# Scan inputs and state products of a hybrid encoder block: one visit of TensorE per block of four array groups, and another split of the PSUM banks

## What is computed

```python
h  = rms_norm(x)
p  = h @ W_in            # [conv x | conv B | conv C | u | gate_a | gate_b]
ya = (B * dwconv3_causal(C * x_conv)) @ W_conv_out
# 32 groups of 16 inputs and 64 complex states:
s_t = A_bar * s_{t-1} + B_bar u_t
yb = GLU(gelu(Re(C s_t) + D u_t))
x  = x + (sigmoid(gate_a) * ya + sigmoid(gate_b) * yb) @ W_o
x  = x + top-2-of-8 experts in the best of 4 groups, of rms_norm(x)
out = rms_norm(x)
```

## Time and profile before

| | us |
|---|---|
| median of three runs | 722.08 |
| lowest, highest | 722.07, 724.77 |
| the profiled execution | 723.69 |
| its span in the trace | 722.0 |
| PE busy, DVE busy in it | 558.9, 206.8 |
| mean granted TensorE clock | 0.89 of full |

### The profile page before, as it was taken

How to read it: one execution, slowest core, us unless ns; L and a number is a source line. 1 busy time by engine, 2 the same in 40 slices (tenths; PEclk the granted TensorE clock), 3 DMA queues, 4 the chain that set the end, 5 groups by cost and what they waited for, 6 DMA issues and landing times.

```text
span 722.0 us, 7544 instructions
## 1 busy us (share of the span) xinstructions
PE 558.9 (77%) x3241; PEld 333.3 (46%) x3241; DVE 206.8 (29%) x443; ACT 70.4 (10%) x132; POOL 39.8 (6%) x68
## 2 busy tenths in 40 slices
PE   8999999999999989899384584566548248457755
PEld 7888888888886646354141141123114014112411
DVE  4799886959512144000010010000001001000002
ACT  3010011111110012100000000000000000000102
POOL 5001111111100011000000000000000000000000
PEclk9999999999999999999796688779679669677889
DMA  9960803363269666999999999999999999999993
GB/s 339 425 268 18 332 1 120 113 242 139 86 270 401 232 235 261 364 432 426 430 428 428 430 427 428 430 428 427 428 429 426 433 428 428 431 426 430 426 426 161
DMA packets 19043, 242.44 MB, mean 336 GB/s; under 512 B 2368, under 2 KB 2496, under 8 KB 4544
## 3 DMA queue, kind: packets, MB, share of 16 engines
q1 hardware_dynamic: 18432, 239.83, 79.8%
q10 hardware_dynamic: 576, 2.10, 0.8%
HBM read 240.87 MB, written 1.05 MB: 335 GB/s over the span
## 4 chain that ended last, share of the span: by engine, by line
PE 54%; DMA 41%; DVE 2%; issue 2%; ACT 0%; POOL 0%; SPq 0%; DVEq 0%; PEldq 0%; POOLq 0%; ACTq 0%
PE bank L1114 27%; DMA ring<-in_w_down 13%; DMA ring<-in_w_gate 12%; PE bank L1364 8%; DMA s_region<-in_w_up 4%; DMA x_region<-in_w_up 4%; PE bank L1372 4%; DMA ring<-in_w_up 4%; PE bank L1246 4%; DMA ring<-in_last_halves 3%; PE bank L1126 2%; PE bank L1413 2%; PE bank L1331 1%; PE bank L1216 1%; PE bank L1231 1%
## 5 line engine op out<-in xcount | busy, mean ns | idle before, releaser
L1364 PE MATMUL bank<-ring,z_region 128*32 128x512 f32 x688 | 118.5, 676 | 63.5 <-DMA ring<-in_w_gate 14.9
L1114 PE MATMUL bank<-x_region,ring 128*128 128x256 f32 x640 | 142.2, 381 | 0.0
L1114 PEld LDWEIGHTS bank<-x_region,ring 128*128 128x128 f32 x640 | 120.4, 190 | 20.9 <-issue 5.1
L1364 PEld LDWEIGHTS bank<-ring,z_region 128*32 128x32 f32 x688 | 33.6, 122 | 123.5 <-issue 123.5
L1372 PE MATMUL bank<-ring,m_region 128*32 128x512 f32 x240 | 55.5, 749 | 26.6 <-DMA ring<-in_w_down 16.0
L1038 DVE TENSOR_TENSOR z_region<-z_region,bank 128x512 f32<-128x512 f32 x8 | 8.2, 1027 | 209.2 <-PE bank L1364 197.1
L1364 PE MATMUL bank<-x_region,z_region 128*32 128x512 f32 x80 | 44.9, 725 | 10.7 <-DMA ring<-in_w_up 10.7
L1042 DVE COPY m_region<-bank 128x512 f32<-128x512 f32 x8 | 5.5, 691 | 139.3 <-PE bank L1372 111.3
L1372 PE MATMUL bank<-s_region,m_region 128*32 128x512 f32 x64 | 36.9, 741 | 8.6 <-DMA ring<-in_w_down 8.6
L1364 PE MATMUL bank<-rot_region,z_region 128*32 128x512 f32 x64 | 37.6, 755 | 6.8 <-DMA ring<-in_w_up 6.8
L1331 PE MATMUL bank<-conv_region,h_region 128*128 128x128 f32 x256 | 33.9, 288 | 4.7 <-issue 4.0
(11 more groups left out here) (240 smaller groups left out, 570.0 us busy)
## 6 DMA issues: line engine op xcount, KB each, us to landing
ring<-in_w_gate SPq DMA_DIRECT2D x26, 2048.0 KB, 34.5
ring<-in_w_up SPq DMA_DIRECT2D x17, 2048.0 KB, 33.8
ring<-in_mix SPq DMA_DIRECT2D x16, 2048.0 KB, 9.7
ring<-in_w_down SPq DMA_DIRECT2D x15, 2048.0 KB, 35.0
ring<-in_first SPq DMA_DIRECT2D x8, 2048.0 KB, 12.6
s_region<-in_w_down SPq DMA_DIRECT2D x4, 2048.0 KB, 36.2
x_region<-in_w_up SPq DMA_DIRECT2D x4, 2048.0 KB, 36.8
rot_region<-in_w_up SPq DMA_DIRECT2D x4, 2048.0 KB, 35.8
```

The costliest lines, as they stand in the source:

```text
L1114: ins = MM(dst, w[:, k, n * P:(n + 1) * P], rhs[:, k, :], start=k == 0, stop=k == kn - 1)
L1364: ins = MM(bank[to][quarter(e), :], xT[:, k, quarter(e)], of_expert[e][:, FF * k:FF * k + FF], start=k == 0, stop=k == KD - 1)
```

## The change

The same products are made, in fewer visits of PE to the scan. Four tables behind mains take the place of the old steps: `array` (scan inputs of a whole block, behind mains 7, 15, 25, 34), `states` (state products of a whole block, behind 20, 26, 35, 45), `behind` (the DVE steps, where they were), `products` (`y_pre` of blocks 0 to 2 behind 22, 31, 40). The gelus of blocks 0 to 2 come behind main 42, and `y_pre` and gelu of block 3 at the very end of the list.

Each visit now has eight products in four array groups: four row groups into banks 4 to 7 (inputs), or four column groups into bank 3 (state products). The projections have banks 0 to 2: x, ga and nearly all gb share bank 0, b and c alternate between 1 and 2, co takes 0, 2, 1 in turn. Six states are kept; two lie where the raw input lay, and the table's scratch moves beside them. The waits follow the banks: x of n = 1, 2 waits for the copy of x(n - 1), x of n > 2 for the sigmoid of gb(n - 3), which stands right before it in the list.

```diff
-S5_LAG = 2
+STATES_KEPT = 6
...
-    order, step = [], 0
+    behind = {7 + t * 9 // 4: ("step", t) for t in range(ST)}
+    products = dict(zip((22, 31, 40), (("ypre", b) for b in range(YB - 1))))
+    array = dict(zip((7, 15, 25, 34), (("bu", b) for b in range(YB))))
+    states = dict(zip((20, 26, 35, 45), (("out", b) for b in range(YB))))
+    order = []
     for g, main in enumerate(mains):
         order.append(main)
-        while step < ST + S5_LAG and g == 7 + step * 9 // 4:
-            order.append(("s5", step))
-            step += 1
-    assert step == ST + S5_LAG
-    return order
+        order += [table[g] for table in (array, states, behind, products) if g in table]
+        if g == 42:
+            order += [("gelu", b) for b in range(YB - 1)]
+    return order + [("ypre", YB - 1), ("gelu", YB - 1)]
...
+        ACT_BANK, Y_BANK, CO_BANKS = 0, 3, (0, 2, 1)
+
+        def conv_bank(j):
+            return 1 + j % 2
+
         def gate_bank(what, n):
 
-            if n + GATE_LAG < KD:
-                return 2 * (n % 2)
-            return 0 if what == "ga" else 2
+            return conv_bank(KD - 2) if what == "gb" and n + GATE_LAG >= KD else ACT_BANK
+
+        def co_bank(n):
+            return CO_BANKS[n % len(CO_BANKS)]
...
+        def state(t):
+
+            t %= STATES_KEPT
+            return s_first[:, t] if t < 4 else s_more[:, t - 4]
...
                 if t >= 2:
                     dve.wait_ge(s_ready, t - 1)
-                if t >= 4:
-                    dve.wait_ge(q_used, t - t % 2 - 2)
-                V.tensor_tensor(s_sb[:, t % 4], zst, cos2, ALU.mult)
+                if t >= STATES_KEPT:
+                    dve.wait_ge(q_used, 4 * ((t - STATES_KEPT) // 4) + 4)
+                V.tensor_tensor(state(t), zst, cos2, ALU.mult)
...
-                    if n >= 4:
-                        pe.wait_ge(ya_ready, n - 3)
+                    if n >= 3:
+                        pe.wait_ge(ya_ready, n - 2)
...
                 unit = U_PARTS[what] + 5 * (n // 4)
-                s = 2 * (n % 2)
                 if what == "x":
+                    if 1 <= n <= GATE_LAG:
+                        pe.wait_ge(xs_ready, n)
+                    elif n > GATE_LAG:
+                        pe.wait_ge(gb_ready, n - GATE_LAG)
+                    dst, done = bank[ACT_BANK][:, 0:T], xbc_psum
+                elif what == "b":
                     if n >= 2:
                         pe.wait_ge(z_ready, n - 1)
-                    if n >= 2 + GATE_LAG:
-                        pe.wait_ge(gb_ready, n - 1 - GATE_LAG)
-                    dst, done = bank[s][:, 0:T], xbc_psum
-                elif what == "b":
-                    dst, done = bank[s + 1][:, 0:T], xbc_psum
+                    dst, done = bank[conv_bank(n)][:, 0:T], xbc_psum
...
                 elif what == "ga":
                     if n + GATE_LAG < KD:
                         pe.wait_ge(xs_ready, n + GATE_LAG + 1)
+                    elif n + GATE_LAG == KD:
+                        pe.wait_ge(gb_ready, n)
                     else:
-                        pe.wait_ge(gb_ready, KD - GATE_LAG - 1)
                         pe.wait_ge(ga_ready, n)
                     dst, done = bank[gate_bank(what, n)][:, 0:T], ga_psum
                 else:
                     if n + GATE_LAG < KD:
                         pe.wait_ge(ga_ready, n + 1)
+                    elif n + GATE_LAG == KD:
+                        pe.wait_ge(z_ready, KD - 1)
                     else:
                         pe.wait_ge(gb_ready, n)
                     dst, done = bank[gate_bank(what, n)][:, 0:T], gb_psum
...
-                if (what, n) == ("x", 1):
-                    pe.wait_ge(u_ready, YB)
...
+            def scan_in(b):
+                if b == 0:
+                    pe.wait_ge(bt_ready, 1)
+                    pe.wait_ge(ct_ready, 1)
+                    pe.wait_ge(u_ready, YB)
+                else:
+                    pe.wait_ge(bu_used, 4 * b)
+                for i in range(2):
+                    for q in range(4):
+                        ins = MM(bank[4 + q][:, i * T:(i + 1) * T], BT[row_tile(q), b, i, :], uT[row_tile(q), b, :],
+                                 start=True, stop=True)
+                ins.then_inc(bu_psum, 4)
+
+            def scan_out(b):
+                if b >= 1:
+                    pe.wait_ge(ypre_ready, b)
+                pe.wait_ge(s_ready, 4 * b + 4)
+                for i in range(2):
+                    for q in range(4):
+                        ins = MM(bank[Y_BANK][row_tile(q), 0:T], CT[:, i, b, row_tile(q)], state(4 * b + q)[:, i, :],
+                                 start=i == 0, stop=i == 1)
+                ins.then_inc(q_used, 4)
...
                 if n < 2:
-                    pe.wait_ge(ya_ready, 6 + 2 * n)
+                    pe.wait_ge(ya_ready, 7 + n)
```

More of the change, by code:

```diff
@@ L162, in block_kernel @@
         h_raw = x_region(0, KD, T)
-        rtmp = x_region(0, 4, T)
+        rtmp = x_region(4 * T, 4, T)
         turned = x_region(4 * T, 2, 2, T)
+        s_more = x_region(0, 2, 2, T)
         extra2 = x_region(0, UNIT)
@@ L173, in block_kernel @@
         zc = h2_region(D, 2, YB, 2, STATE)
-        s_sb = h2_region(0, 4, 2, T)
+        s_first = h2_region(0, 4, 2, T)
         h2 = h2_region(0, TB, KD, P)
@@ L529, in state_sums @@
             def state_sums(t):
-                s, sp = s_sb[:, t % 4], sprod[:, t % 2]
+                s, sp = state(t), sprod[:, t % 2]
                 pool.wait_ge(q_ready, t + 1)
@@ L597, in main @@
                         act.wait_ge(z_ready, n - 1)
-                    nc.scalar.activation(xs[:, n % 2, :], bank[2 * (n % 2)][:, 0:T], ACT.Copy).then_inc(xs_ready, 1)
+                    nc.scalar.activation(xs[:, n % 2, :], bank[ACT_BANK][:, 0:T], ACT.Copy).then_inc(xs_ready, 1)
                 elif what == "ga":
@@ L606, in main @@
                                          bias=cols[:, R_GATEB + KD + n:R_GATEB + KD + n + 1]).then_inc(gb_ready, 1)
[L608 to L612, removed]
             def gelu(b):
@@ L618, in _ @@
             for what, n in SCHEDULE:
-                s5(n) if what == "s5" else main(what, n)
+                gelu(n) if what == "gelu" else main(what, n)
             act.wait_ge(s_ready, ST)
+            act.wait_ge(q_used, 12)
             act.wait_ge(rot_ready, YB)
@@ L820, in conv @@
                 dve.wait_ge(xbc_psum, 3 * j + 3)
-                link(V.tensor_tensor(v_sb[:, s, 2:T + 2], bank[2 * s + 1][:, T:2 * T], xs[:, s, :], ALU.mult))
+                link(V.tensor_tensor(v_sb[:, s, 2:T + 2], bank[conv_bank(j)][:, T:2 * T], xs[:, s, :], ALU.mult))
                 link(V.tensor_scalar(ct[:, 0, :], v_sb[:, s, 2:T + 2], w[2], cols[:, R_CONVB + j:R_CONVB + j + 1],
@@ L825, in conv @@
                 link(V.scalar_tensor_tensor(ct[:, 0, :], v_sb[:, s, 0:T], w[0], ct[:, 1, :], ALU.mult, ALU.add))
-                V.tensor_tensor(z_sb[:, j, :], bank[2 * s + 1][:, 0:T], ct[:, 0, :], ALU.mult).then_inc(z_ready, 1)
+                V.tensor_tensor(z_sb[:, j, :], bank[conv_bank(j)][:, 0:T], ct[:, 0, :], ALU.mult).then_inc(z_ready, 1)
                 dve.wait_ge(z_ready, j + 1)
@@ L894, in s5_step @@
                 dve.wait_ge(bu_psum, t + 1)
-                bu = bank[4 + t % 2][:].rearrange("p (i t) -> p i t", i=2)
+                bu = bank[4 + t % 4][:].rearrange("p (i t) -> p i t", i=2)
                 cos2, sin2 = (w.unsqueeze(1).to_broadcast([P, 2, T]) for w in (cos, sin))
@@ L918, in y_pre @@
                 V.scalar_tensor_tensor(yT[:, b, :], uT[:, b, :], cols[:, R_SSMD + b:R_SSMD + b + 1],
-                                       bank[6 + b % 2][:, 0:T], ALU.mult, ALU.add).then_inc(ypre_ready, 1)
+                                       bank[Y_BANK][:, 0:T], ALU.mult, ALU.add).then_inc(ypre_ready, 1)
             def main(what, n):
@@ L926, in main @@
                     dve.wait_ge(ga_ready, n + 1)
[L927 to L935, removed]
-            for what, n in SCHEDULE:
-                s5(n) if what == "s5" else main(what, n)
+                    V.tensor_tensor(mixed[:, n, :], bank[co_bank(n)][:, 0:T], mixed[:, n, :], ALU.mult).then_inc(ya_ready, 1)
+            for what, n in SCHEDULE:
+                if what == "step":
+                    s5_step(n)
+                elif what == "ypre":
+                    y_pre(n)
+                else:
+                    main(what, n)
             dve.wait_ge(gb_ready, KD)
@@ L1164, in main @@
                         pe.wait_ge(gb_ready, KD)
-                    if n >= 4:
-                        pe.wait_ge(ya_ready, n - 3)
+                    if n >= 3:
+                        pe.wait_ge(ya_ready, n - 2)
                     mix_loaded(pe, U_CO + n // 4)
-                    project(bank[n % 4][:, 0:T], w8(U_CO + n // 4), n % 4, z_sb, ya_psum, arrives=z_ready if n == 0 else None)
```

(30 more changed lines are left out.)

## The result

| | before | after |
|---|---|---|
| median, us (10 runs each) | 723.88 | 718.25 |
| lowest, highest | 722.07, 724.77 | 717.06, 720.76 |
| profiled execution, span | 723.69, 722.0 | 717.06, 715.3 |

The ratio is 0.9928, 95% interval 0.9912 to 0.9943: 5.6 us, 0.8% faster. The forecast was 5.64 us less, and 716.4 us.

What follows compares the result with a forecast made beforehand. PE's mixer path was taken to bound the kernel, us for us. Visits saved 9.80 us, less waits of 0.84, 1.62 and 1.70, gave 5.64 us off the median of 722.08: 716.4 us, range 714.3 to 720.1.

Steps and rivals of the forecast that it cites:

- What bounds: From the first main to the GLU, PE's time sets when the expert stream starts and ends, each us at full worth.
- The visits, 9.80 us: In the mixer, half of eight input visits (1.26 us each) and eight state visits (1.19 each) go: 9.80 us removed.
- Four row groups: Input visits: whether products in four row groups all overlap; a round takes 0.22, 0.43 or 0.86 us.
- The low end: Input visits: all four row groups overlap, 0.22 us a round; the bound the forecast took.
- the other two ends: Input visits: row groups overlap two at a time (0.43 us a round, 720.0 us, chance 0.08) or not at all (0.86).
- The slower rival: Input visits: four row groups don't overlap at all, 10.6 us more, 727.0 us; chance 0.04.
- The waits: Added PE waits: three in the mixer (0.84 us, and 0.81 twice) and one behind it (1.70 us).
- x(1) 0.74: Mixer: x(1) waits for x(0)'s copy, 0.74 us and about 0.10 for a weight load, 0.84 us.
- gb(0) and gb(4): Mixer: x(3) and x(7) wait for the sigmoids of gb(0) and gb(4), 0.71 + 0.10 us each, 1.62 us.
- behind the mixer: Before the GLU, PE waits for co(7)'s multiply, y_pre and gelu of block 3: 1.60 + 0.10 = 1.70 us.
- DVE's cover, 3.2 us: Behind main 34, DVE's chain has 3.2 us left before co(4) waits; rival of a late DVE 718.4 us, chance 0.07.
- The term of either sign: Clock fall at 269.4 us, behind PE's wait for the second norm, may move or vanish: 1.7 us both ways.

Runs made afterwards that it cites:

- four waits gone: Changed kernel with block 3's y_pre and gelu behind main 45, x(1) and x(3) in bank 3, block 1's state products behind main 30: 713.59 us median.
- input visits split: Changed kernel with each input visit of eight products made two visits of four, the second behind the next main: 723.19 us median, ratio 0.9991.
- six multiplications: Changed kernel with six unread multiplications, 7.5 us in all, added on DVE ahead of scan step 12: 721.79 us median, ratio 0.9968.

## Why the prediction was right

- **What bounds.** PE's path in the mixer, us for us to the end: four waits gone gave 4.04 us at the GLU and 4.7 in the median; two slowed kernels (input visits split, six multiplications) gave 4.6 and 4.3 at the GLU, counted from x(1), and 4.9 and 3.5 in the median. Right, within the 1 us or so by which medians of so few executions go astray.
- **The visits, 9.80 us.** 9.7 with all waits away; the visits with twice the products cost 0.01 to 0.02 us more each, which is the missing 0.1.
- **Four row groups.** The open bound of the sum. The low end (0.22 us a round) was right, and the other two ends had the right visits: 1.93 us for two groups, 3.65 for one. The slower rival as a whole was under-priced, 10.6 us against 18.1 measured (18.7 at the GLU), since it left out that the clock falls.
- **The waits.** x(1) 0.74, gb(0) and gb(4) 0.73 each (worked out 0.71), behind the mixer 1.52 (worked out 1.60), each with a weight load of 0.10 in the open. 4.1 us against 4.16. The wait behind the mixer is avoidable, as are the other three, so the change as made takes 5.6 us of the 9.7 that it could.
- **DVE's cover, 3.2 us.** Right within what was tried. The prediction put the next wait at co(4); with six multiplications co(3) waited first, which was expected before that run but not in the prediction.
- **The term of either sign.** I gave it 1.7 us both ways; it is 1.0 to 1.5, there or not there. The first 0.42 us of that sum was taken over a microsecond in which PE was busy for only 0.29, so some of it may have been no cost; that was not tested.
- **How exact it was.** That the medians differ by 5.63 us where 5.64 was forecast is luck to the tenth: the interval of the ratio allows 4.1 to 6.4 us. At the GLU, too, 5.65 us comes of small misses that cancel: the visits saved 0.1 less, the last wait was 0.1 shorter, and its weight load falls behind that point.
- **The base.** The time came out at 718.25 and not 716.4, though the difference was right: the three executions of before had a median of 722.08, ten had 723.88. A forecast from the profiled execution, 718.1, would have been nearer, since that one happened to lie at the median of the ten.

## What to carry over

Price a visit of TensorE to another shape of tiles by its edge and its rounds, not by its products: filling a visit up to four array groups is nearly free, and one visit fewer saves all of it (here 1.2 us). Before giving up banks for that, walk the list and look which main stands directly behind the read-out of its own bank; those few places can be covered, as they were here, by moving a visit there or by a bank that is idle at that time. And never move the last link of a chain behind the work that covered it, even where the list reads tidier.

## What the hardware showed that was not expected

- Products of different row groups don't wait for each other in the order of the list: with each group's two products side by side in the list the visit took 1.10 us against 1.08.
- The granted clock fell to 1.2 GHz without PE having been idle, at visits whose products used one row group of the array (K = 32) for 3.65 us, at four visits out of four, and that cost 8.4 us in all; not at visits of 1.93 us with two groups, nor of 1.08 us with four. Which of the two it was, the length or the single group, is not settled: no run varied one alone.
- Where two visits of different tile shapes touch, the edge of 0.20 us is paid once: with the input visits split, two of the four added visits stood beside a state visit, and the GLU came 4.6 us later where four edges would have made it 5.0.
